# Two of every eight gathered value rows summed on VectorE instead of TensorE

## The reference

```python
def block(xb):                      # 128 tokens
    ...
    eid = e1 * PEER_NKEYS + e2      # 8 heads x 16 experts per token
    gate = jax.nn.softmax(sc, axis=-1)
    hid = jnp.einsum('thkd,td->thk', expert_u[eid], xb, preferred_element_type=f32)
    act = jax.nn.gelu(hid, approximate=False) * gate
    return jnp.einsum('thk,thkd->td', act, expert_v[eid].astype(f32)).astype(xb.dtype)
```

## Time and profile before

| | |
|---|---|
| Time, median of 3 runs | 4106.42 us (4103.27 to 4132.05) |
| Profiled execution, span from first to last instruction | 4090.1 us |
| PE busy | 3315.7 us, 81% of the span |
| DVE busy | 2191.8 us, 54% |
| ACT busy | 992.4 us, 24% |
| POOL busy | 2278.2 us, 56% |
| Moved by DMA | 1214 MB, of which 1073.87 MB by POOL's queue |
| TensorE's granted clock, mean | 0.888 of full speed |
| Stage B with experts | from 524 us on |

### The profile page before, as it was taken

One profiled execution on the slowest core, in us unless ns is written; L12 is line 12 of the kernel. 1 busy time (PEld: TensorE's weight loads), 2 busy tenths in 40 slices (PEclk: granted clock), 3 DMA queues, 4 the chain that ended last, 5 costly groups with the idle time before them and its releaser, 6 DMA issues.

```text
span 4090.1 us, 38210 instructions
## 1 busy us (share of the span) xinstructions
PE 3315.7 (81%) x11032; PEld 1816.9 (44%) x11032; DVE 2191.8 (54%) x4881; ACT 992.4 (24%) x2278; POOL 2278.2 (56%) x2189
## 2 busy tenths in 40 slices
PE   8997757897788787887879778877888687969999
PEld 4444535453444344443535344444545253534444
DVE  1124285567444854477456744486357644574543
ACT  2112213222222132212221222212221222213332
POOL 0000055667556775767566755676566656666764
PEclk9998778898889897898889888898899798989999
DMA  3321187899789998899889978899799979999996
GB/s 125 118 75 63 39 298 263 309 363 389 264 302 335 362 358 289 316 346 365 280 313 373 365 269 297 318 360 342 278 324 369 356 260 322 352 364 373 381 355 243
DMA packets 413927, 1214.00 MB, mean 297 GB/s; under 512 B 43680, under 2 KB 137888, under 8 KB 413600
## 3 DMA queue, kind: packets, MB, share of 16 engines
q0 software_dynamic: 294912, 1073.87, 71.6%
q1 hardware_dynamic: 118816, 137.66, 9.9%
HBM read 1190.61 MB, written 20.77 MB: 296 GB/s over the span
## 4 chain that ended last, share of the span: by engine, by line
PE 54%; DVE 14%; issue 13%; DMA 7%; POOL 5%; ACT 4%; another core or an unknown queue 2%; SPq 1%; POOLq 0%; DVEq 0%; ACTq 0%
PE expert_sum L894 28%; PE bank L894 23%; DVE u_rows L1645 5%; DMA u_rows<-in_peer_u_dram,group_ids 4%; DMA w_query<-in_peer_w_query_dram 3%; PE bank L897 3%; POOL u_rows L576 3%; POOL v_rows L576 2%; ACT weight_diagonals L610 1%; ACT L610 1%; ACT arena L610 1%; DVE arena L1420 1%; DVE arena L1552 1%; DVE arena L1537 1%
## 5 line engine op out<-in xcount | busy, mean ns | idle before, releaser
L894 PE MATMUL expert_sum<-v_rows,weight_diagonals 128*128 128x512 f32 x4096 | 1871.7, 617 | 153.0 <-ACT weight_diagonals L610 116.9
L576 POOL DMA_INDIRECT v_rows<-in_peer_v_dram,group_ids x1024 | 1191.1, 1163 | 827.7 <-PE expert_sum L894 541.8
L1645 DVE CUSTOM_DVE_ANT_0 u_rows<-u_rows,ffn_in 128x1024 f32<-128x1024 f32 x1024 | 1215.7, 1225 | 454.8 <-DMA u_rows<-in_peer_u_dram,group_ids 410.3
L894 PEld LDWEIGHTS expert_sum<-v_rows,weight_diagonals 128*128 128x128 f32 x4096 | 810.4, 200 | 1161.7 <-issue 1078.0
L576 POOL DMA_INDIRECT u_rows<-in_peer_u_dram,group_ids x1024 | 1052.3, 1028 | 416.8 <-issue 371.0
L897 PE MATMUL bank<-constants,arena 128*128 128x128 f32 x968 | 184.5, 336 | 330.2 <-DVE arena L1475 82.4
L610 ACT ACTIVATE weight_diagonals<-constants,expert_weight 128x128 f32<-128x128 f32 x1024 | 331.7, 390 | 228.5 <-PE expert_sum L894 177.4
L894 PE MATMUL bank<-w_query,arena 128*128 128x256 f32 (+1 forms) x1088 | 297.6, 436 | 87.4 <-DMA w_query<-in_peer_w_query_dram 50.6
L610 ACT ACTIVATE gelu<-hidden 128x8 f32<-128x8 f32 x128 | 26.7, 208 | 1386.1 <-DVE hidden L1645 1237.0
L897 PEld LDWEIGHTS bank<-constants,arena 128*128 128x128 f32 x968 | 139.1, 171 | 392.6 <-issue 212.2
L894 PEld LDWEIGHTS bank<-w_query,arena 128*128 128x128 f32 x1088 | 231.6, 215 | 155.7 <-issue 59.6
(11 more groups left out here) (166 smaller groups left out, 1968.1 us busy)
## 6 DMA issues: line engine op xcount, KB each, us to landing
w_query<-in_peer_w_query_dram SPq DMA_DIRECT2D x64, 1024.0 KB
u_rows<-in_peer_u_dram,group_ids POOLq DMA_INDIRECT x1024
v_rows<-in_peer_v_dram,group_ids POOLq DMA_INDIRECT x1024
w_channel<-in_w_in_dram SPq DMA_DIRECT2D x12, 512.0 KB
conv_scratch<-conv_out SPq DMA_DIRECT2D x12, 512.0 KB, 2.6
arena<-conv_scratch SPq DMA_DIRECT2D x8, 768.0 KB
tok_scratch<-token_out SPq DMA_DIRECT2D x8, 648.0 KB
arena<-tok_scratch SPq DMA_DIRECT2D x8, 648.0 KB
```

The lines of the kernel that those rows point to most:

```text
L576: nc.gpsimd.indirect_dma_start(ring[:, j, :], None, table, bass.IndirectOffsetOnAxis(ids[:, half, j:j + 1], 0)).then_inc(landed[j], 16)
L894: return nc.tensor.matmul(out_, lhsT, rhs, start=start, stop=stop, **kw)
L1645: v.tensor_tensor_reduce(u_ring[:, j, :], u_ring[:, j, :], xb[:], 1.0, 0.0, ALU.mult, ALU.add, hid[:, g * G + j:g * G + j + 1]).then_inc(u ...
```

## The change

Of the 8 rows of v in a group, rows 3 and 7 (`ON_DVE`) are no longer summed by PE. DVE multiplies each with its weight and adds it to `rest_sum`, a tile in SBUF (`add_rows`); the first one of a pass is written without an add. The other six (`ON_PE`) stay with PE, and ACT makes six diagonals. At the end of a pass `experts_out` adds `rest_sum` and PE's sum. On DVE the adds of group g-1 come after the dots and weights of group g and before piece g; those of the last group come ahead of `publish`. POOL, before it gathers v rows 2 and 3, and before 6 and 7, also waits until DVE has added row 3 or row 7 of the group before (`v_added`); its other waits count only PE's six rows. To make room for `rest_sum`, the tile `onehot` of the search is halved and used twice, and `mixT` moves to another place of the arena.

```diff
+ON_PE = (0, 1, 2, 4, 5, 6)
+ON_DVE = (3, 7)
+NPE, NDVE = len(ON_PE), len(ON_DVE)
...
-            diag = sb(b_ctx, "weight_diagonals", [P, G, P])
+            diag = sb(b_ctx, "weight_diagonals", [P, NPE, P])
...
-        mixT = part(45.25, 8 * P).rearrange("p (s n) -> p s n", n=P)
+        mixT = part(37.25, 8 * P).rearrange("p (s n) -> p s n", n=P)
...
-        onehot = part(41.25, 2 * D).rearrange("p (h k a) -> p h k a", h=PH, k=TOPK)
+        onehot = part(41.25, D).rearrange("p (h k a) -> p h k a", h=PH // 2, k=TOPK)
+        rest_sum = part(45.25, D)
...
+                before = t * NG + g - 1
...
+                for j in range(G):
+                    if j % 2 == 0 and not first:
+
+                        pool.wait_ge(u_used, before * G + j + 2)
+                        pool.sem_inc(wait_carrier)
+                    nc.gpsimd.indirect_dma_start(
+                        u_ring[:, j, :], None, table_u, bass.IndirectOffsetOnAxis(ids[:, half, j:j + 1], 0)).then_inc(u_landed[j], 16)
+                for j in range(G):
+                    if j % 2 == 0 and not first:
+
+                        pool.wait_ge(v_used, before * NPE + len([i for i in ON_PE if i <= j + 1]))
+                        pool.sem_inc(wait_carrier)
+                        if j + 1 in ON_DVE:
+
+                            pool.wait_ge(v_added, before * NDVE + ON_DVE.index(j + 1) + 1)
                             pool.sem_inc(wait_carrier)
...
+                    nc.gpsimd.indirect_dma_start(
+                        v_ring[:, j, :], None, table_v, bass.IndirectOffsetOnAxis(ids[:, half, j:j + 1], 0)).then_inc(v_landed[j], 16)
...
-                for j in range(G):
+                for i, j in enumerate(ON_PE):
                     pe.wait_ge(v_landed[j], (t * NG + g + 1) * 16)
-                    pe.wait_ge(diag_ready, t * SLOTS + g * G + j + 1)
+                    pe.wait_ge(diag_ready, (t * NG + g) * NPE + i + 1)
                     for n in range(2):
-                        last = mm(acc[:, n * 512:n * 512 + 512], diag[:, j, :], v_ring[:, j, n * 512:n * 512 + 512],
-                                  False, g == NG - 1 and j == G - 1)
+                        last = mm(acc[:, n * 512:n * 512 + 512], diag[:, i, :], v_ring[:, j, n * 512:n * 512 + 512],
+                                  False, g == NG - 1 and i == NPE - 1)
...
+            def add_rows(t, g):
+
+                for i, j in enumerate(ON_DVE):
+                    dve.wait_ge(v_landed[j], (t * NG + g + 1) * 16)
+                    weight = act_w[:, g * G + j:g * G + j + 1]
+                    if g == 0 and i == 0:
+
+                        dve.wait_ge(weights_ready, t * NG + 1)
+                        ins = v.tensor_scalar(rest_sum, v_ring[:, j, :], weight, None, ALU.mult)
+                    else:
+                        dve.wait_ge(v_added, (t * NG + g) * NDVE + i)
+                        ins = v.scalar_tensor_tensor(rest_sum, v_ring[:, j, :], weight, rest_sum, ALU.mult, ALU.add)
+                    ins.then_inc(v_added, 1)
+
             def experts_out(t):
 
-                dve.wait_ge(v_used, (t + 1) * SLOTS)
+                dve.wait_ge(v_used, (t + 1) * NG * NPE)
+                dve.wait_ge(v_added, (t + 1) * NG * NDVE)
                 for n in range(2):
-                    v.tensor_copy(h2_sb[:, n * 512:n * 512 + 512], acc[:, n * 512:n * 512 + 512]).then_inc(h2_ready, 1)
+                    half = slice(n * 512, n * 512 + 512)
+                    v.tensor_tensor(h2_sb[:, half], rest_sum[:, half], acc[:, half], ALU.add).then_inc(h2_ready, 1)
 
             def tile(t):
                 for g in range(NG):
                     experts(t - 1, g)
                     if g == 0:
                         experts_out(t - 2)
+                    else:
+                        add_rows(t - 1, g - 1)
                     pieces[g](t)
+                add_rows(t - 1, NG - 1)
                 publish(t)
```

More of the change, by code:

```diff
@@ L818, in experts @@
                 act.wait_ge(weights_ready, t * NG + g + 1)
-                for j in range(G):
+                for i, j in enumerate(ON_PE):
                     if not (isinstance(t, int) and t == 0 and g == 0):
-                        act.wait_ge(v_used, t * SLOTS + (g - 1) * G + j + 1)
-                    f(diag[:, j, :], ident, ACT.Copy, scale=act_w[:, g * G + j:g * G + j + 1]).then_inc(diag_ready, 1)
+                        act.wait_ge(v_used, (t * NG + g - 1) * NPE + i + 1)
+                    f(diag[:, i, :], ident, ACT.Copy, scale=act_w[:, g * G + j:g * G + j + 1]).then_inc(diag_ready, 1)
             for piece in pieces[:10]:
@@ L1572, in pick @@
             def pick(t, h0, nh):
+                hot = onehot[:, 0:nh]
                 hs, cols = slice(h0, h0 + nh), slice(h0 * TOPK, (h0 + nh) * TOPK)
@@ L1586, in pick @@
                     dve.wait_ge(vector_step, steps(t))
-                    v.tensor_tensor(onehot[:, hs].rearrange("p h k a -> p (h k) a"),
+                    v.tensor_tensor(hot.rearrange("p h k a -> p (h k) a"),
                                     cst[:, C_IOTA:C_IOTA + TOPK].unsqueeze(1).broadcast_to([P, nh * TOPK, TOPK]),
@@ L1593, in pick @@
                     by_half = key_numbers.rearrange("p (h f) k -> p f h k", f=2)[:, half]
-                    v.tensor_tensor(onehot[:, hs], onehot[:, hs], by_half.unsqueeze(2).broadcast_to([P, nh, TOPK, TOPK]),
+                    v.tensor_tensor(hot, hot, by_half.unsqueeze(2).broadcast_to([P, nh, TOPK, TOPK]),
                                     ALU.mult).then_inc(vector_step, 1)
                     dve.wait_ge(vector_step, steps(t))
-                    v.reduce_sum(e_half[:, half, cols], onehot[:, hs].rearrange("p h k a -> p (h k) a"),
+                    v.reduce_sum(e_half[:, half, cols], hot.rearrange("p h k a -> p (h k) a"),
                                  AX.X).then_inc(vector_step, 1)
@@ L1678, in _ @@
             experts(0, 1)
+            add_rows(0, 0)
             best_pair(0, 3)
@@ L1688, in _ @@
                 experts(0, FIRST + i)
+                add_rows(0, FIRST + i - 1)
                 for piece in group:
                     piece(1)
+            add_rows(0, NG - 1)
             publish(1)
@@ L1725, in _ @@
                 k = (g - 1) // 2
+                if g:
+                    add_rows(NT - 1, g - 1)
                 if g == 0:
@@ L1735, in _ @@
                     normed_rows(k + 1)
+            add_rows(NT - 1, NG - 1)
             experts_out(NT - 1)
```

7 lines of the change are left out of this document (1 added, 6 removed).

## The result

The changed kernel takes 4452.32 us (median of 4 runs, 4435.19 to 4457.12); the kernel before took 4108.36 on the same chip (4103.27 to 4132.05). The ratio is 1.080, 95% interval 1.076 to 1.085: 8% slower, where 4364 was forecast with a range of 4235 to 4490. The profiled execution after has a span of 4455.3 us with a mean granted TensorE clock of 0.815 (before: 4090.1 and 0.888).

A forecast was written before the change was run, and what follows sets the result against it. PE and the DMA engines were taken as both near full. Passes 1 to 6 +170, last pass +65 and +3, pass 0 +20, sum +258: span 4090.1 to 4348, plus 16.3 for the median, 4364 us; range 4235 to 4490.

The forecast's parts named there:

- The new wait on GpSimd: v rows 2 to 7 of g wait for the row 3 add of g-1, behind the dots of g: 28.7 us a turn.
- The turn: One round of the ring per group: 27.05 + 1.34 + 0.3 = 28.7 us, low 27.6, high 30.1.
- the stretch from third v gather to next weights: Largest part of a turn, read from the trace before: 27.05 us in the last pass, 27.97 in pass 3.
- the ring: Closed loop per group: add, six v gathers, ids, eight u gathers, landing, last dot, gelu, weights, add; sets some 88 turns.
- The sum over a pass: Pass 3 from weights to weights: 473.1 us for 438.8; passes 1 to 6 given all 474, together +170.
- PE, removed: Two of 8 rows leave PE's diagonal matmuls: 468 us of 1872 busy time, 286 us of it on the path.
- DVE, added: Two operations of 1284 ns a group, 329 us in all; hidden under PE's burst, costing 2.6 us where DVE is late.
- PE's saving through: Rival: PE's shorter bursts shorten the kernel, 4106 - 286 plus 57 for adds, 3877 us; chance 0.03.
- The faster ring: Rival: empty queue lands v rows sooner, turn 27.0 us: 4214, chance 0.09; with free pass boundary 4145, chance 0.03.
- DVE holds up GpSimd: Rival: gathers beside DVE's adds and front pieces stretch, two of 1.03 us in 88 turns, +181, 4545 us; chance 0.08.
- The stretched row: Last-pass gather taking 1.99 us instead of 0.97, read as a two-SBUF-operand DVE dot holding GpSimd up by about 1 us.
- Signs foretold: If right: DVE releases v gathers, turns about 28.7 us, last-pass DMA share near 0.83, PE busy down some 468 us.

The follow-up runs named there:

- e2: Kernel before, all rows on PE, no adds; GpSimd also waits for the weights of g before the third v gather of g: 4394.52 us, ratio 1.080.
- e1: Changed kernel, but VectorE adds rows 3 and 7 of group g-1 ahead of the dots of g: 4167.15 us, ratio 1.026.
- e4: Changed kernel with rows 5 and 7 on VectorE instead of 3 and 7: 4158.2 us, one run, ratio 1.022.
- e10: Changed kernel with rows 1 and 7 on VectorE instead of 3 and 7: 4598.42 us, ratio 1.190.
- e11: Changed kernel with row 7 alone on VectorE, seven rows on PE: 3914.17 us, ratio 1.013.
- e6: Kernel before, PE summing all 8 rows; VectorE also adds a constant tile twice a group, no wait on an add: 4233.83 us, ratio 1.025.
- e8: Changed kernel, adds behind the dots, but each add except the first of a pass works on 8 columns: 4420.68 us, ratio 1.070.
- e3: Changed kernel, but adds read a constant tile instead of rows 3 and 7, and GpSimd waits for no add: 4199.51 us, one run, 1.03 times the kernel before.
- e7: Changed kernel with adds ahead of the dots, each add except the first of a pass on 8 columns: 4222.34 us, ratio 1.022.
- e12: Repeat of e1, changed kernel with adds of g-1 ahead of the dots of g: 4193.78 us, ratio 1.029.
- e5: Changed kernel, but VectorE takes rows 5 and 7 only in 42 of 128 groups, PE all 8 elsewhere: 4086.61 us, ratio 0.988.
- e9: Same as e5 but rows 6 and 7 on VectorE in the same 42 groups: 3857.2 us, ratio 0.998.

## Why the prediction was right, step by step

*The new wait on GpSimd* was the step that decided, and it held: e2 shows that it alone makes the kernel 8% slower, e1 that the same work in another order loses only a third of that, e4, e10 and e11 that the turn follows the number of gathers ahead of the wait.

*The turn.* 28.7 us was forecast, 29.1 measured (407.9 / 14). For the stretch from third v gather to next weights 27.05 was forecast and 29.1 − 2.0 = 27.1 measured, but that it fits so well is luck. The prediction took group 14's, which is the shortest of the last pass before; group 9's, for one, was 3923.61 + 0.17 − 3893.79 = 29.99:
```profile
3893.79 1.38 POOL L576 DMA_INDIRECT v_rows<-in_peer_v_dram,group_ids  x1 [0.30 <-issue]
```
```profile
3923.61 0.17 DVE L1648 TENSOR_TENSOR expert_weight<-gelu,gate 128x8 f32<-128x8 f32 x1 [0.27 <-issue]
```
The fourteen before had a mean of 28.5, the fourteen after have one of 27.2 (25.6 to 28.8). So the stretch did get 1.3 us shorter with the ring, as the prediction feared among its signs of being wrong; from the mean it would have forecast a turn of 30.2. The rest was 1.64 (add 1.34, wake-up 0.3) and is 2.0: the wake-up takes 0.76, the upper bound that I gave. The last pass came to +71 for +65, its first two groups to +3 for +3.

*The sum over a pass was mis-sized.* Pass 3 by its pieces, forecast and measured (from the weights above): group 15 to 1, 52 and 56.0; 1 to 5, 114.8 and 113.9; 5 to 6, 34 and 36.3; 6 to 12, 175.8 and 184.5; 12 to 15, 96.5 and 96.1. Together 473.1 and 486.7. In the first of these the 30.7 us of the ring came out at 32.0 and the 21.3 of the group that only gathers, for which no row was shown, at 24.0; the terms of the last add up to 96.2 and not 96.5. Nearly two thirds of the miss, 8.7 us, are in 6 to 12, where I let the w_query loads lengthen only the last turn (they share the DMA engines, not the queue, as the prediction has it); the trace after has turns of 32.8, 30.4, 29.7, 28.8, 32.7 and 30.1 us there. The two long ones are those in which SyncE starts one of the eight loads (at 2217.8) and three (2335.9 to 2355.2); that the loads make them long is argued, not shown. Passes 1 to 6 take 486.3 on average where I gave all 474: 6 x 12.3 = 74 us too little. Pass 0 was never dissected: +40 in place of +20. With 6 from the last pass this is 100 of the 107 us between the forecast span of 4348 and 4455.

*PE, removed.* The term was wrongly written: 1024 x 617 ns is 632 us, not 468. 468 is a quarter of the busy time of 1872 us, in which records overlap, and the argument used that one. Busy time of the diagonal matmuls fell by 380 us (1871.7 to 1491.4), since one record now takes 643 ns at a lower clock; PE's whole busy time fell by 306. None of it came through.

*DVE, added.* 1286 ns each for 1284 forecast. That it costs only where VectorE is late is what e6 shows in the main (+104 us for 330), and e8 puts its share in the changed kernel at about 1 of 8 per cent.

*The rivals.* PE's saving through: fell. The faster ring: fell at its price, 29.1 for 27.0, though the stretch in it did get shorter. DVE holds up GpSimd: its price fell, its mechanism stood. The stretched row was read rightly. The first gather behind the wait runs beside the second add and takes 1.39 us in place of 0.94 (e8 above); in the whole trace after, the 165 gathers that meet an add in their first 0.94 us take 1.33 us on average, the 528 that meet only a dot 1.22, the other 1355 0.96. The cost is 0.45 us a turn and not twice 1.03: some 40 us over 88 turns, my estimate. The sum had it only as far as the 27.05 us that it used held one stretched gather. The page's means hide this: they went from 1163 to 1081 ns per gather (v) and from 1028 to 1036 (u), because 740 gathers met a dot before and only 528 after. In e8 a gather beside an operation of stage C with one operand in PSUM (L1756, from 4366.39 on) keeps its 0.94 us, and the next one, beside an operation with both operands in SBUF (L1759), takes 1.55. The Trainium skill's inference (SBUF — State Buffer, "Who interferes with whom") that writing descriptors is not held up by VectorE instructions with two SBUF inputs does not agree with these rows, and the rows decide.

*Signs foretold.* Releaser of GpSimd's waits, third v gather 1.6 to 2.2 us after the weights (2.0), weights some 28.7 us apart (29.1) and DMA share in the last pass near 0.83 (0.82) are as said; PE's busy time fell by 306 us and not by 468. The clock fell to 0.815; I had named that as what would lift the time above my reasons. In e2 the clock is 0.92 in the last pass and the loss the same, so the loss does not need the deeper fall; what the fall costs beside it no run shows alone.

*What stays open.* With the ring open (e1, e3, e7, e12) the kernel is still 2 to 3% slower than before, though PE is busy with diagonal matmuls for 1440 to 1458 us in place of 1872 and, in e7, VectorE next to nothing more. PE's clock (0.83 for 0.888), the adds' place ahead of the dots in e1 and the stall below may each have a part. I could not divide it, since no run of this order met a chip without the stall. Where it lies can be read: of the 66 us by which e1's span is longer than that of before, pass 0 has 35 and passes 1 to 6 have 42, while the last pass is 3 shorter and the stretches before and behind the passes together 8. e10's 1.190 and the others' ratios on that chip may not be laid beside the rest to the last per cent for the same reason.

## What to carry to other kernels

When an edit moves the release of a buffer to another engine, ask where in that engine's order the releasing instruction stands, and whether anything ahead of it needs what is queued behind the wait: here the closed ring cost 8%, and freeing the busiest engine of a quarter of a stage's matmuls gave nothing. In the last pass it could give nothing, since the DMA engines were at 0.98 already. The length of such a ring can be read in the trace of the kernel before, from the issue to the next release. Take all turns and not one: here they had 27.0 to 30.0 us, and once the ring was closed 25.6 to 28.8. Then count every other transfer in the queue inside each turn. If rows must be freed late, give the late releaser the last ones in the queue (e4, e11), or only those groups in which the ring has room (e5: 1.2% faster than before, e9: 0.2%).

## What the hardware showed that I had not expected

The experiments met four chips. Three of them (e1 to e4, e5 to e8, e12) hold VectorE up in a way that the fourth (e9 to e11) does not; the profiles of before and after show it too. ACT has such waits as well (92 us in the kernel before, 144 after). In e7 a row of the front piece starts 11 us after the matmuls that release it, while VectorE and PE are both idle and GpSimd issues 8 u gathers in a row; it starts 2 us after the last of them. VectorE's and GpSimd's timelines in e7:
```profile
1170.35 0.74 DVE L1444 TENSOR_TENSOR arena<-arena,bank 64x256 f32<-64x256 f32 x2 [11.25 <-remote]
1183.17 0.43 DVE L1447 TENSOR_TENSOR gdn_state<-gdn_state,small 128x256 f32<-128x256 f32 x1 [12.07 <-remote]
```
```profile
1171.31 0.96 POOL L580 DMA_INDIRECT u_rows<-in_peer_u_dram,group_ids  x1 [0.99 <-POOL group_ids L572]
...
1180.04 0.94 POOL L580 DMA_INDIRECT u_rows<-in_peer_u_dram,group_ids  x1 [0.30 <-issue]
```
The profile puts the release down to another core or an unknown queue. The same row's waits in the kernel before, in the changed one, and in e11, which ran on the fourth chip:
```profile
DVE gdn_state L1432 <- remote: 50.8, 6, 8.5
```
```profile
DVE gdn_state L1447 <- remote: 77.4, 10, 11.5
```
```profile
DVE gdn_state L1447 <- PE bank L909: 17.3, 16, 1.3
```
On that chip no engine has a wait of this kind in e9, e10 or e11, and the kernel before takes 3866 us in place of 4069 to 4129. In e4 only three are left on this row (17.3 us), and its slots 4 to 6 take 76.8 us where the kernel before takes 98.3. What is waited for I could not find. One guess is that the next instructions are being fetched behind the gathers; but in none of the six stalls of this row in the kernel before does a packet of the two instruction queues (part 3 of the page) start, which speaks against it. Which slot meets the stall depends on when the gathers run, so that a per cent between two such kernels may be chance of place; e4's 1.022 beside e1's 1.026 is such a pair.
